# Two-layer decoder block on one core: layer one's probabilities transposed through a DRAM scratch, conv taps shared with ScalarE, memory squares loaded in halves

## The reference, cut to what matters

```python
proj = x @ w_in + b_in                     # 256 x 2048 by 2048 x 5376
c_val, c_glu, c_gate, q, k, v, a_gate = split(proj)
# conv branch: 1024 channels, 31 causal taps a channel
h = c_val * sigmoid(c_glu)
h = depthwise_conv(h, conv_w) + conv_b     # sum over 31 taps
y_conv = silu(layer_norm(h)) * silu(c_gate)
# attention: 16 heads of 64, 2 kv heads, blocks of 128, window 128, a sink a head
p = exp(scores - m); probs = p / (sum(p) + exp(sink - m))
y_attn = (probs @ v) * silu(a_gate)
y = layer_norm(ALPHA * x + concat(y_conv, y_attn) @ w_out + b_out)
```

## Time and profile before

| | us |
|---|---|
| three runs | 1606.83, 1607.77, 1608.21; median 1607.77 |
| the profiled execution, its own time | 1610.55 |
| its span, first to last instruction | 1608.8 |
| TensorE busy in the span | 1600.3 (99%) |
| VectorE busy | 1056.6 (66%) |
| ScalarE busy | 785.7 (49%) |
| GpSimd busy | 114.5 (7%) |
| mean share of the 16 DMA engines used by weights and other hardware queues | 56.6% |

### The profile page before, as it was taken

How to read it: one execution, slowest core, us unless ns; L and a number is a source line. 1 busy time by engine, 2 the same in 40 slices (tenths; PEclk the granted TensorE clock), 3 DMA queues, 4 the chain that set the end, 5 groups by cost and what they waited for, 6 DMA issues and landing times.

```text
span 1608.8 us, 23677 instructions
## 1 busy us (share of the span) xinstructions
PE 1600.3 (99%) x8859; PEld 1360.5 (85%) x8859; DVE 1056.6 (66%) x1493; ACT 785.7 (49%) x1096; POOL 114.5 (7%) x187
## 2 busy tenths in 40 slices
PE   8999999999999999999999999999999999999999
PEld 8999889888877988788888888888888888888887
DVE  5989898789765767976666655555554555555554
ACT  4455664655534565664564644444443344444432
POOL 3000000310100000000000011111100001111100
PEclk9999999999999999999999999999999999999999
DMA  9655445698576554358554566666656557666663
GB/s 307 220 163 190 138 154 168 184 306 303 195 268 202 151 168 131 120 170 306 186 174 154 167 229 209 225 218 214 216 197 198 194 184 233 210 221 222 212 205 107
DMA packets 174428, 322.63 MB, mean 201 GB/s; under 512 B 7971, under 2 KB 44113, under 8 KB 173184
## 3 DMA queue, kind: packets, MB, share of 16 engines
q1 hardware_dynamic: 167184, 298.05, 56.6%
q0 software_dynamic: 7152, 23.33, 4.5%
HBM read 308.76 MB, written 12.58 MB: 200 GB/s over the span
## 4 chain that ended last, share of the span: by engine, by line
PE 99%; DMA 1%; SPq 0%; DVE 0%; ACT 0%; issue 0%; DVEq 0%
PE ps_g L395 27%; PE ps_g L397 26%; PE ps_g L396 26%; PE ps_g L440 4%; PE ps_g L442 4%; PE ps_g L441 4%; PE ps_m L318 1%; DMA raw<-in_w_in_dram 1%; PE ps_m L1123 0%; PE ps_m L1182 0%; PE ps_m L983 0%; PE ps_m L1104 0%; PE ps_g L416 0%; PE ps_g L414 0%; PE ps_g L415 0%; PE ps_m L1190 0%
## 5 line engine op out<-in xcount | busy, mean ns | idle before, releaser
L471 DVE TENSOR_TENSOR lo<-raw,hi 128x1024 fp32r<-128x1024 f32 (+3 forms) x551 | 650.2, 1184 | 462.3 <-ACT hi L456 455.7
L456 ACT CAST hi<-raw 128x1024 fp32r<-128x1024 f32 (+3 forms) x551 | 561.5, 1021 | 718.6 <-PE ps_g L397 616.1
L395 PE MATMUL ps_g<-hi,aH 128*128 128x512 f32 (+3 forms) x1376 | 529.1, 384 | 0.0
L397 PE MATMUL ps_g<-hi,aL 128*128 128x512 f32 (+3 forms) x1376 | 519.9, 378 | 0.0
L396 PE MATMUL ps_g<-lo,aH 128*128 128x512 f32 (+3 forms) x1376 | 519.3, 377 | 0.0
L395 PEld LDWEIGHTS ps_g<-hi,aH 128*128 128x128 f32 x1376 | 258.8, 188 | 48.9 <-issue 3.2
L397 PEld LDWEIGHTS ps_g<-hi,aL 128*128 128x128 f32 x1376 | 258.6, 188 | 48.7
L396 PEld LDWEIGHTS ps_g<-lo,aH 128*128 128x128 f32 x1376 | 259.0, 188 | 46.1 <-issue 0.5
L440 PE MATMUL ps_g<-aH,hi 128*128 128x256 f32 x512 | 147.5, 288 | 3.2 <-DVE lo L471 2.2
L442 PE MATMUL ps_g<-aH,lo 128*128 128x256 f32 x512 | 145.5, 284 | 0.0
L441 PE MATMUL ps_g<-aL,hi 128*128 128x256 f32 x512 | 145.5, 284 | 0.0
(11 more groups left out here) (423 smaller groups left out, 1366.3 us busy)
## 6 DMA issues: line engine op xcount, KB each, us to landing
raw<-in_w_gu_dram SPq DMA_DIRECT2D x88, 1024.0 KB, 5.0
raw<-in_w_in_dram SPq DMA_DIRECT2D x60, 1024.0 KB, 5.1
raw<-in_w_down_dram SPq DMA_DIRECT2D x44, 1024.0 KB, 5.1
raw<-in_w_out_dram SPq DMA_DIRECT2D x32, 1024.0 KB, 5.3
raw<-in_w_in_dram SPq DMA_DIRECT2D x42, 512.0 KB, 4.9
raw<-in_w_ck_dram SPq DMA_DIRECT2D x8, 1024.0 KB, 5.5
raw<-in_w_cv_dram SPq DMA_DIRECT2D x8, 1024.0 KB, 5.3
turned<-hb POOLq DMA_DIRECT2D x88, 64.0 KB, 4.5
```

The costliest lines, as they stand in the source:

```text
L395: pe.matmul(dst, xh, wh, start=first, stop=False)
L397: last = pe.matmul(dst, xl, wh, start=False, stop=final)
L456: act.copy(step_view(hi, s), raw_view(s)).then_inc(s_hi, 1)
L471: dve.tensor_tensor(step_view(lo, s), raw_view(s), step_view(hi, s).bitcast(F32), ALU.subtract).then_inc(s_lo, 1)
```

## The change

1. Probabilities of a pair are no longer transposed by PE. DVE transposes them in blocks of 32x32 (`probs_blocks`, slot s + 3, one instruction of 128x768 a pair), POOL stores the blocks in four DMAs to a DRAM scratch `turned1` and loads them back, transposed, in one DMA. `probs_T` and `probs_copy` go. `pv` moves to slots s + 10 and s + 11, `normalize` to s + 13. The scratch, `sB` and `pT` are double buffered. `pv` now writes one of two PSUM banks by pair.
2. Later slots for what follows: GATE is 69 and 79 (was 67 and 74) and its PE, ACT and DVE parts come two slots later behind it; LN is 86 (was 83), and everything counted from LN moves with it.
3. Convolution: ACT makes the first tap of every channel tile (`first_tap`); for groups 0, 1 and 3 ACT also begins a second sum `acc` with tap 1 and makes products of the odd taps 3 to 29 in a double buffer `prod`; DVE adds the even taps as before, adds a product to the second sum (two tiles at once, 128x512), and joins the sums at the end. Group 2 goes by taps on DVE. DVE has 150 taps, 42 additions and 3 joins, ACT 98 instructions of 128x256. Units a slot follow a new table (`conv_rate`).
4. The memory squares are loaded in two halves of 32 DMAs: k-tiles 8 to 15 once the second channel sums are done, k-tiles 0 to 7 once the conv branch is gated.
5. `mem_rows` lies at another place in SBUF, so its load waits on SP for the parameter columns (`s_cols`).

```diff
+            for u in range(HEADS // 2):
+                pool.wait_ge(s_pb, u + 1)
+                if u >= 2:
+                    pool.wait_ge(s_pr, 16 * (u - 1))
+                for q in range(4):
+                    pool.dma_start(turned1[u % 2, :, :, :, q, :].rearrange("b r x c -> r x b c"),
+                                   sB[32 * q:32 * q + 32, u % 2].rearrange("r (x b c) -> r x b c", x=6, b=4)
+                                   ).then_inc(s_pw, 16)
+                pool.wait_ge(s_pw, 16 * 4 * (u + 1))
+                if u >= 2:
+                    pool.wait_ge(s_pv, 2 * u - 2)
+                pool.dma_start(pT[:, u % 2].rearrange("p x t -> p (x t)"),
+                               turned1[u % 2].rearrange("b r x q c -> (b r) (x q c)")).then_inc(s_pr, 16)
+            for half in (1, 0):
+                if half == 1:
+                    pool.wait_ge(s_lns, 3)
+                else:
+                    pool.wait_ge(s_lng, 4)
+                    pool.wait_ge(s_conv, len(conv_units))
...
-        SM, EX, PT, PV, NM = 1, 2, 3, 5, 7
-        GATE = [G["ag1"]["s0"] + 3, G["ga0"]["s0"] + 2]
-        LN = G["ga1"]["s0"] + 3
+        SM, EX, TB, PV, NM = 1, 2, 3, 10, 13
+        GATE = [G["ag1"]["s0"] + 5, G["ga0"]["s0"] + 7]
+        LN = G["ga1"]["s0"] + 6
...
+        def conv_rate(p):
+            kv = G["kv"]["s0"]
+            if 9 <= p < kv or G["ag1"]["s0"] <= p < LN:
+                return 3
+            return 2 + p % 2 if after_kv <= p < G["ag1"]["s0"] else 0
...
-            def probs_T(u, h):
...
             def pv(u, h):
-                n = 2 * u + h
-                pe.wait_ge(s_pTc, n + 1)
-                if u >= 1:
-                    pe.wait_ge(s_yn, u)
+                pe.wait_ge(s_pr, 16 * (u + 1))
+                if u >= 2:
+                    pe.wait_ge(s_yn, u - 1)
...
                     if p == LN:
                         channel_parts(0, cT)
                     if p == LN + 1:
                         channel_mean(0)
-                    if p == LN + 3:
-                        channel_parts(1, sq_sb)
-                    if p == LN + 4:
-                        channel_mean(1)
...
             for g in groups[11:17]:
                 for j in range(g["ns"]):
                     gemm(pe, g, j, y_operand(yaH, aH[:, 8:]), y_operand(yaL, aL[:, 8:]), before_wo(g))
+                    if g["s0"] + j == LN + 3:
+                        channel_parts(1, sq_sb)
+                    if g["s0"] + j == LN + 4:
+                        channel_mean(1)
...
+            def products(p):
+                for i in conv_slot.get(p, ()):
...
+                    for c in range(2):
+                        last = act.activation(prod[:, n % 2, c, :], hT[:, 2 * j + c, tap:tap + T], ACT.Copy,
+                                              scale=convw[:, 2 * j + c, tap:tap + 1])
+                    last.then_inc(s_prod, 1)
...
+            def probs_blocks(u):
+                b = 2 * (u % 2)
+                dve.wait_ge(s_exp, u + 1)
+                if u >= 2:
+                    dve.wait_ge(s_pw, 16 * 4 * (u - 1))
+                dve.transpose(sB[:, u % 2], sS[:, b:b + 2, :].rearrange("p h c -> p (h c)")).then_inc(s_pb, 1)
```

More of the change, by code:

```diff
@@ L491, in stack_kernel @@
         sS = put("sS", 160.25, [P, 4, 3 * P])
-        pT = put("pT", 190, [P, 2, 3 * P])
+        pT = put("pT", 190, [P, 2, 6, P])
+        sB = put("sB", 196, [P, 2, 6 * P])
+        turned1 = nc.dram_tensor("turned1", (2, 4, 32, 6, 4, 32), F32, kind="Internal").ap()
         k_dup = put("k_dup", 163.25, [P, TT, KVH, 2, HD])
@@ L616, in stack_kernel @@
         memT0 = put("memT0", 118, [P, 2, T])
-        mem_rows = put("mem_rows", 190, [P, TT, D])
+        mem_rows = put("mem_rows", 112, [P, TT, D])
         mH = put("mH", 144, [P, KT, T], F32R)
@@ L717, in keys_lo @@
             return keysL[k // 8][:, k % 8:k % 8 + n, :]
-        conv_units = 8 * TAPS
+        conv_units, BY_TAPS = [], 2
+        for j in range(4):
+            if j == BY_TAPS:
+                conv_units += [("tap", j, tap, c) for tap in range(1, TAPS) for c in range(2)]
+                continue
+            for m in range(TAPS // 2):
+                if m:
+                    conv_units.append(("add", j, 2 * m + 1, None))
+                conv_units += [("tap", j, 2 * m + 2, c) for c in range(2)]
+            conv_units.append(("join", j, None, None))
+        product_at = [i for i, u in enumerate(conv_units) if u[0] == "add"]
+        with_products = [j for j in range(4) if j != BY_TAPS]
+        acc = put("acc", 132, [P, 2, 2, T])
+        prod = put("prod", 203.75, [P, 2, 2, T])
+        s_acc = sem("conv_second_sum_begun")
+        s_prod = sem("conv_products")
         def memT(k, n):
@@ L872, in _ @@
             window_mask()
[L873 to L878, removed]
+            for u in range(HEADS // 2):
[17 more added lines that the diff above has]
+                    pool.wait_ge(s_conv, len(conv_units))
+                ks = slice(8 * half, 8 * half + 8)
+                for b in range(4):
+                    for s in range(2 * 4):
+                        pool.dma_start(memB[32 * b:32 * b + 32, ks, 32 * s:32 * s + 32],
+                                       a["mem_2"][0][32 * s:32 * s + 32, :].rearrange(
+                                           "c (k b r) -> b c k r", k=KT, b=4)[b, :, ks]).then_inc(s_mem, 16)
             pool.wait_ge(s_xl, built("mem", KT))
@@ L1521, in conv_gate, with first_tap @@
                 last.then_inc(s_stga, 1)
+            def first_tap(j):
+                evacuated(act, G[f"cm{j}"])
+                act.wait_ge(s_pad, 1)
+                act.wait_ge(s_colsb, 2)
+                for ct in (2 * j, 2 * j + 1):
+                    act.activation(cT[:, ct, :], hT[:, ct, 0:T], ACT.Identity, scale=convw[:, ct, 0:1],
+                                   bias=cols[:, CB + ct:CB + ct + 1]).then_inc(s_tap0, 1)
+                if j == BY_TAPS:
+                    return
+                r = with_products.index(j)
+                if r >= 2:
+                    act.wait_ge(s_conv, conv_units.index(("join", with_products[r - 2], None, None)) + 1)
+                for c in range(2):
+                    last = act.activation(acc[:, r % 2, c, :], hT[:, 2 * j + c, 1:1 + T], ACT.Copy,
+                                          scale=convw[:, 2 * j + c, 1:2])
+                last.then_inc(s_acc, 1)
+            def products(p):
+                for i in conv_slot.get(p, ()):
+                    if i not in product_at:
+                        continue
+                    n, (_, j, tap, _) = product_at.index(i), conv_units[i]
+                    if tap == 3:
+                        act.wait_ge(s_pad, 1)
+                        act.wait_ge(s_colsb, 2)
+                        evacuated(act, G[f"cm{j}"])
+                    if n >= 2:
+                        act.wait_ge(s_conv, product_at[n - 2] + 1)
+                    for c in range(2):
+                        last = act.activation(prod[:, n % 2, c, :], hT[:, 2 * j + c, tap:tap + T], ACT.Copy,
+                                              scale=convw[:, 2 * j + c, tap:tap + 1])
+                    last.then_inc(s_prod, 1)
             def columns(name, dst, func, b):
@@ L2188, in _ @@
                 if p == LN:
-                    conv(conv_units - conv_at[0])
+                    conv(p)
                 if p == LN + 2:
```

123 lines of the change are left out of this document (58 added, 65 removed).

## The result

| | before | after |
|---|---|---|
| median of 21 runs, us | 1608.14 | 1611.64 |
| lowest and highest | 1606.83, 1610.64 | 1608.35, 1614.11 |
| profiled execution, its own time | 1610.55 | 1610.88 |
| its span | 1608.8 | 1609.2 |

The ratio is 1.0020 (95% interval 1.0014 to 1.0026): the change makes the kernel slower, by 3.5 us between the medians. Forecast were 1605.5 us, a range of 1602.4 to 1610.5 and "slower" with a chance of 0.12. Sign and range are both missed. The interval is about 1 us to each side, where the prediction took 3.2 us for the least that can be told.

A forecast was written before the change was run, and what follows sets the result against it. In layer one TensorE's own instruction list was taken as the bound. Transposes -5.0 and the second mean's wait +2.7 gave -2.3 us, all else nothing: 1605.5 us against the median of 1607.77, range 1602.4 to 1610.5.

The forecast's parts named there:

- "slower" with a chance of 0.12: Whole kernel: measured slower than before, chance 0.12, beside 0.28 for faster and 0.60 for same.
- Transposes off PE: Layer-one attention on PE: removing the probability transposes saves 0.32 us a head over 16 heads, gain 5.0 us.
- The second mean: Layer norm's channel_mean(1): PE newly waits for ACT's copy of the sums, behind ga1's evacuation; loss 2.7 us.
- The rule weighed there: Table loads ahead of the sums copy: a 1.38 us drain behind each makes the loss 5.5; rival at 1608.3 us, chance 0.05.
- The step that failed: VectorE: Conv work on DVE: falls back about 1 us from some 9 us of lead, then catches up; nothing on PE.
- DRAM round trip: POOL's stores and load of probabilities: 15 to 16 us, in time for PE's values; cost nothing.
- the slack: Time between the load of pair 1 landing and PE wanting it at 170.8: 8.6 us.
- Rival 3: POOL's round trip is the bound, lateness adding up over seven pairs to 7.5 us of waits at L1035; 1613 us, chance 0.10.
- Weights and squares: Later weight loads after the moved wo0 bias step, beside halved square DMAs: nothing taken; ends 0.3 us gained, 4 lost.
- the other bound of 4: Weights and squares: the losing end kept for the later weight loads beside squares in halves, 4 us lost.

The follow-up runs named there:

- Experiments 5: The change with LN in slot 87, VectorE's center and conv_rstd ahead of the slot's lo, ga1 evacuated after the first sums copy, earlier wo0 bias step: 1604.37 us.
- 10: The re-ordered chain of Experiments 5 with LN back in slot 86: 1607.66 us.
- experiment 9: The change with four product buffers in place of two for conv group 3, and ScalarE's products of that group two slots earlier: 1610.26 us.
- experiment 7: The change with all four conv groups by taps on VectorE, four units a slot, three in steps 40 to 63: 1609.99 us.
- Experiment 4: The kernel before with three more 128x1024 copies on ScalarE ahead of the copy of the second channel sums: 1611.42 us, ratio 1.0020.
- Experiment 6: The change with its part 4 undone, all memory squares loaded in one piece after conv_lo as before: 1615.42 us.
- number 12: The kernel before with center and conv_rstd with the first scale ahead of the slot's lo on VectorE: 1608.16 us, ratio 0.9997.
- 2: The change with all four conv groups split between VectorE's taps and ScalarE's products, two units a slot in steps 40 to 63: 1611.26 us.
- numbers 1: The change with ScalarE's evacuation of ga1 behind the copy of the second channel sums, not ahead of it: 1609.85 us.
- number 8: The change with four conv units a slot from step 64 on, not three: 1618.73 us.
- number 11: The re-ordered chain of Experiments 5 with center and conv_rstd behind their slot's lo, as in the change: 1606.61 us.

## Why the prediction was wrong

**Transposes off PE: right.** 5.0 us forecast, 4.9 measured; a pair's three steps in cm3 take 169.99 - 159.06 = 10.93 us where 11.0 was forecast and the earlier trace rows show 11.61.

**The second mean: right.** 2.7 forecast, 2.5 measured, through the very rows named. The rule weighed there (the Trainium skill, ScalarE: Activation LUTs, What ACT_TABLE_LOAD costs) does not hold in this trace either: the load of 288.37 ends at 289.65 and the first activation starts at 289.67, so there is no drain of 1.38 us behind it; the sum by the row was the better one.

**The step that failed: VectorE.** "DVE falls back by about 1 us, out of a lead of up to three steps, some 9 us. After it, a slot holds two taps and one addition in place of four taps, and DVE catches up. Nothing on PE." The 9 us were the lead at steps 48 to 64. In the earlier trace rows VectorE idled 5.1 us in 93, which is some 94% busy; I took that for a margin, when it says that each us taken off PE's list comes out of VectorE's time as well. It lost 3.7 us of free time up to step 86. Its lead at step 64 was 3.5 us where before had 7.8, a fall of 4.3 and not of 1; it started the last stretch with 2.1 us of lead and not 7.8, and had 96% of work in it, so it did not catch up. The cost at the join, put at nothing, was a wait of 2.6 us. The last unit stands in slot 85 with the sums in 86, the same distance as before (82 and 83), where it was made with 0.2 us to spare. A column of VectorE's lead by step against the deadline would have shown it; I counted the work and not the deadline. Experiments 5 and 10 show that the join comes at its own time and that asking a step later takes the wait away (3.3 us). Why it comes so late is read from the traces and not settled by a run: less free time, the second gate's copies in slot 84, and ScalarE's waits for product buffers (0.5 us by experiment 9, at least) may each have a part, and experiment 7, where the last tap was in time, changed load, products and the place of the last unit at once.

**What no term had: the clock.** The sum priced a wait at its length. Experiment 4 measured 3.4 us for 2.2 of wait. With 5.1 us of new waits the runs' clock is 0.998 in the median where before has 1.000, and by the table that is 2.8 of the 3.5 us. The prediction read 0.999 in the profile of before and did not ask what it was.

**DRAM round trip: right that it costs nothing; the slack agrees by luck.** The load of pair 1 landed 8.2 us before its use, where 8.6 were forecast, but two errors of over 4 us cancel in that. From the first store to the landing it took 11.5 us and not 15 to 16, and PE wanted the values at 165.9 and not at 170.8: the start of this execution was 1.6 us quicker, and PE had gained 3.8 us by step 55, not the 1 allowed for. The stores of the pairs start 9.4 to 11.7 us apart. Rival 3 is out: no wait at L1035.

**Weights and squares: right.** Nothing was forecast, and 0.3 us were gained, the end that the bounds had. Experiment 6, with the squares in one piece, came to 3.8 us, near the other bound of 4, which was put on the squares in halves.

Corrected sum: -4.9 + 2.5 + 2.6 + 0.5 - 0.3 = +0.4, where 0.7 was measured at equal clock. The slow clock adds 2.1 to 3.0 by the count above: 2.5 to 3.4 against 3.5.

## What to carry to other kernels

When one engine is the bound and the next is 92 to 96% busy, work taken from the first moves every deadline of the second earlier: compute the second one's lead step by step up to its next fixed deadline, not its share. Take the waits out by asking later or by placing the chain ahead of routine work in the list; a control like number 12 tells whether the order or the saved work pays. And price a wait of PE above its length, as experiment 4 measured it (3.4 us for 2.2).

## What was not expected of the hardware

Behind a wait of TensorE of 2.1 to 2.6 us the granted clock may be 0.50 (1.2 GHz) for 3.4 us, then 1.00 again. It is not certain: in the profiles of numbers 6 and 9 it came behind both waits, in those of 2 and 7 at the wait on the mean alone, in those of numbers 1, 4 and 10 behind none. In number 8 the wait of 2.4 us on lo had one behind it, and those of 1.9, 1.6 and 1.4 us had none; nor had the one of 2.0 us in number 11. Windows of number 9 (clock ahead of the last two columns):

```profile
276.60:280.00 3.40, 3.40 (x18) 3.40 (x18) 0.84 (x1) 0.21 (x1) 0.00 (x0) 0.50 0.72 223
...
293.60:297.00 3.40, 3.40 (x9) 2.68 (x9) 2.92 (x4) 2.28 (x3) 3.40 (x7) 0.51 0.45 123
```

What decides between the two in an execution stays open; no run here varied the length of the wait alone.
